# A depthwise convolution moved from 93 VectorE taps and 31 TensorE taps to 128 column-group matmuls

## What is computed

```python
def conv_module(val, gate, w_dw, b_dw, ln_g, ln_b):
    u = val * jax.nn.sigmoid(gate)                      # 512 channels
    u = lax.conv_general_dilated(u, w_dw[:, None, :], window_strides=(1,), padding=[(15, 15)],
                                 feature_group_count=512) + b_dw          # depthwise, 31 taps
    return jax.nn.silu(layernorm(u, ln_g, ln_b))        # over the 512 channels
```

## Time and profile before

| | us |
|---|---|
| median of three timed runs | 1810.6 (1808.02 to 1812.49) |
| the profiled execution, own time | 1805.73 |
| span of its trace | 1804.0 |
| PE busy in the span | 1754.0 (97%) |
| DVE busy | 1133.6 (63%) |
| ACT busy | 622.3 (34%) |
| POOL busy | 94.5 (5%) |

### The profile page before, as it was taken

One profiled execution on the slowest core, in us unless ns is written; L12 is line 12 of the kernel. 1 busy time (PEld: TensorE's weight loads), 2 busy tenths in 40 slices (PEclk: granted clock), 3 DMA queues, 4 the chain that ended last, 5 costly groups with the idle time before them and its releaser, 6 DMA issues.

```text
span 1804.0 us, 23419 instructions
## 1 busy us (share of the span) xinstructions
PE 1754.0 (97%) x9247; PEld 1469.9 (81%) x9247; DVE 1133.6 (63%) x1736; ACT 622.3 (34%) x842; POOL 94.5 (5%) x164
## 2 busy tenths in 40 slices
PE   8999999999998999999999999999999999899997
PEld 5888888888645788888888888888888989899997
DVE  5578667876885657866787577323346446665554
ACT  5322222233575432212223322122223333454343
POOL 0010000110120001000010000000000000000000
PEclk8999999999999999999999999999999999999999
DMA  9455555552101245555655353232222222245553
GB/s 392 163 196 174 188 166 198 173 181 96 45 7 42 70 140 195 176 187 166 197 173 165 119 196 128 96 114 93 73 92 94 71 71 94 94 163 170 181 170 110
DMA packets 49040, 253.36 MB, mean 140 GB/s; under 512 B 5568, under 2 KB 7104, under 8 KB 32576
## 3 DMA queue, kind: packets, MB, share of 16 engines
q1 hardware_dynamic: 30384, 184.10, 29.8%
q0 software_dynamic: 18576, 68.17, 12.1%
HBM read 251.20 MB, written 1.05 MB: 140 GB/s over the span
## 4 chain that ended last, share of the span: by engine, by line
PE 91%; DVE 4%; ACT 3%; DMA 1%; issue 1%; SPq 0%; ACTq 0%; DVEq 0%
PE ps L521 28%; PE ps L523 28%; PE ps L522 28%; PE ps L924 1%; DVE w_lo L1412 1%; PE ps L953 1%; ACT w_hi L1056 1%; PE ps L580 1%; DMA mod_raw<-in_mod_first 1%; DVE t_ring L1482 1%; PE ps L771 1%; DVE hn_lo L1489 0%; PE ps L551 0%; PE ps L785 0%; PE ps L757 0%
## 5 line engine op out<-in xcount | busy, mean ns | idle before, releaser
L521 PE MATMUL ps<-hn_hi,w_hi 128*128 128x512 f32 (+2 forms) x1784 | 643.9, 361 | 10.5 <-DVE hn_lo L1489 7.5
L523 PE MATMUL ps<-hn_hi,w_lo 128*128 128x512 f32 (+2 forms) x1784 | 637.4, 357 | 0.0
L522 PE MATMUL ps<-hn_lo,w_hi 128*128 128x512 f32 (+2 forms) x1784 | 637.3, 357 | 0.0
L1412 DVE TENSOR_TENSOR w_lo<-raw,w_hi 128x2048 fp32r<-128x2048 f32 (+2 forms) x179 | 365.6, 2042 | 334.9 <-ACT w_hi L1056 334.7
L1056 ACT ACTIVATE w_hi<-raw 128x2048 fp32r<-128x2048 f32 (+2 forms) x179 | 307.0, 1715 | 713.9 <-PE ps L523 710.6
L521 PEld LDWEIGHTS ps<-hn_hi,w_hi 128*128 128x128 f32 (+1 forms) x1784 | 337.1, 189 | 68.2 <-DVE hn_lo L1489 10.1
L523 PEld LDWEIGHTS ps<-hn_hi,w_lo 128*128 128x128 f32 (+1 forms) x1784 | 337.0, 189 | 49.7
L522 PEld LDWEIGHTS ps<-hn_lo,w_hi 128*128 128x128 f32 (+1 forms) x1784 | 337.2, 189 | 47.7 <-issue 0.5
L521 PE MATMUL ps<-a_hi,w_hi 128*128 128x512 f32 (+1 forms) x704 | 255.4, 363 | 1.7 <-DVE a_lo L1558 1.7
L522 PE MATMUL ps<-a_lo,w_hi 128*128 128x512 f32 (+1 forms) x704 | 255.2, 362 | 0.0
L523 PE MATMUL ps<-a_hi,w_lo 128*128 128x512 f32 (+1 forms) x704 | 255.2, 362 | 0.0
(11 more groups left out here) (220 smaller groups left out, 1264.5 us busy)
## 6 DMA issues: line engine op xcount, KB each, us to landing
raw<-in_w_up SPq DMA_DIRECT2D x88, 1024.0 KB, 5.0
mod_raw<-in_mod_w POOLq DMA_DIRECT2D x128, 512.0 KB, 3.9
raw<-in_w_downA SPq DMA_DIRECT2D x32, 768.0 KB, 4.2
raw<-in_w_downB SPq DMA_DIRECT2D x32, 640.0 KB, 3.9
raw<-in_w_od_in SPq DMA_DIRECT2D x16, 1024.0 KB, 5.0
mod_raw<-in_mod_first SPq DMA_DIRECT2D x8, 1024.0 KB, 11.9
raw<-in_w_ev_in SPq DMA_DIRECT2D x7, 1024.0 KB, 4.9
raw<-in_w_ev_out SPq DMA_DIRECT2D x4, 1024.0 KB, 5.0
```

What stands on the lines that cost most here:

```text
L521: pe.matmul(o, lh, rh, start=first, stop=False)
L522: pe.matmul(o, lh, rl, start=False, stop=False)
L523: return pe.matmul(o, ll, rh, start=False, stop=last)
L1412: dve.tensor_tensor(w_lo[:, u0 % 2, 0:n], raw[:, u0 % 2, 0:n], w_hi[:, u0 % 2, 0:n], ALU.subtract).then_inc(lo_made, 1)
```

## The change

All four channel tiles of the convolution go to PE, in another form, and DVE and ACT no longer compute it.

- **Form.** A tile of 128 channels is cut in four groups g of 32 channels. For group g the 128 rows of the array hold 4 taps by 32 channels, its 32 columns the 32 output channels. Group g writes PSUM partitions 32g to 32g+31, so that the four groups use the four column groups of the array. Eight steps i cover 4 x 8 = 32 taps (the 32nd is zero): step i takes tap 8q+i from row block q. So a tile is 8 x 4 = 32 matmuls of 128 rows, 32 columns and 512 moving columns; four tiles are 128 matmuls.
- **Shifted copies.** Row block q of group g needs the group's 32 channels shifted by 8q. SP makes them with DMAs inside SBUF: 16 per tile (`shift_tile`), each 32 partitions x 2 streams x 263 floats (67,328 bytes), into `mod_raw`, two tiles deep. SP issues them for tile 0 after the load of unit E+4, for tile 1 after that of E+5, and for tiles 2 and 3 after the second load of the output projection, behind waits on `conv_mm` 1 and 2 (a tile's last matmul).
- **Weights.** POOL lays each tile's taps out as [128, 32, 32] with one product of an identity and the taps (`lay_taps`, four instructions instead of 31).
- **PE.** `conv_part(n)` replaces `conv_turn(n)` at the same place: two steps (8 matmuls) in each of the 16 loop steps.
- **Copy out.** DVE copies each tile from PSUM with the bias (`conv_out`) at j = 5, 9, 13 and 17.
- **Rows of the conditioning vectors.** `mod_raw` must be free meanwhile, so POOL stops at row 54 (before: 60), and loads rows 54 to 59 after the last tile's matmuls.

```diff
-        EARLY = 30
-        TAP_ORDER = [(n % 2, n // 2) for n in range(EARLY + 12)]
-        for _n in range(10):
-            TAP_ORDER += [(2, 2 * _n), (0, 21 + _n), (2, 2 * _n + 1), (1, 21 + _n)]
-        TAP_ORDER += [(2, _n) for _n in range(20, CONV_W)]
-        TAPS = len(TAP_ORDER)
-        TAP_AT = {tap: n for n, tap in enumerate(TAP_ORDER)}
-        AHEAD_OF_LOOP = EARLY + 11
...
+        SHIFTS = TAP_ROWS * 2 * REACH
+        flat = mod_raw[:].rearrange("p a b -> p (a b)")
+
+        def shifted_place(c):
+            at = c % 2 * SHIFTS
+            return flat[:, at:at + SHIFTS].rearrange("p (g s n) -> p g s n", g=4, s=2)
+
+        def taps_place(c):
+            place = wide[:, 0:2, :].rearrange("p a b -> p (a b)") if c % 2 == 0 else flat[:, 2 * SHIFTS:2 * SHIFTS + 1024]
+            return place.rearrange("p (g i j) -> p g i j", g=4, i=TAP_STEPS)
+
+        def conv_bank(c):
+            return 1 if c % 2 == 0 else 3
+
+        def conv_parts(j):
+            return range(2 * (j - 1), 2 * j) if 1 <= j <= len(ATT) else range(0)
...
+            def shift_tile(c):
+
+                sp.wait_ge(unit_evac, U["ev_in"] + (1, 2, 6, 7)[c])
+                sp.wait_ge(pad_clear, 1)
+                if c >= 2:
+                    sp.wait_ge(conv_mm, c - 1)
+                for g in range(4):
+                    for q in range(TAP_ROWS):
+                        at = q * TAP_STEPS
+                        sp.dma_start(shifted_place(c)[32 * q:32 * q + 32, g], upad[32 * g:32 * g + 32, c, :, at:at + REACH])\
+                            .then_inc(shifted[c % 2], 16)
+
             for i in range(2, 7):
                 load(U["ev_in"] + i, 0, 0, t["w_ev_in"][i], UNIT)
+                if i == 4:
+                    sp.wait_ge(mod_made, KT + MOD_F0)
+                if i in (4, 5):
+                    shift_tile(i - 4)
             for i in range(4):
                 load(U["ev_out"] + i, 0, 0, t["w_ev_out"][i], UNIT)
+                if i == 1:
+                    shift_tile(2)
+                    shift_tile(3)
...
-            for i in range(SLOTS_MOD, MOD_F0 + SLOTS_MOD):
+            for i in range(SLOTS_MOD, MOD_F0):
...
+            def lay_taps(c):
+
+                eye = col("eye", 0, 32).unsqueeze(1).to_broadcast([P, 32, 32])
+                taps = col("conv_w", 32 * c, 32).unsqueeze(2).to_broadcast([P, 32, 32])
+                pool.tensor_tensor(taps_place(c).rearrange("p g i j -> p (g i) j"), eye, taps, ALU.mult)\
+                    .then_inc(taps_laid, 1)
+
             pool.wait_ge(rstd_mm, 2)
-            for n in range(CONV_W):
-                if n >= DIAGS:
-                    pool.wait_ge(turned_tap, n - DIAGS + 1)
-                pool.tensor_scalar(diag_place(n), ident, col("conv_w", n * CT + 3), None, ALU.mult).then_inc(diag_ready, 1)
-            for i in range(MOD_F0 + SLOTS_MOD, NMOD):
-                pool.wait_ge(mod_made, KT + i - SLOTS_MOD + 1)
+            lay_taps(0)
+            pool.wait_ge(mod_made, KT + MOD_F0)
+            lay_taps(1)
+            for c in range(2, CT):
+                pool.wait_ge(conv_mm, c - 1)
+                lay_taps(c)
+            pool.wait_ge(conv_mm, CT)
+            for i in range(MOD_F0, NMOD):
+                if i >= MOD_F0 + SLOTS_MOD:
+                    pool.wait_ge(mod_made, KT + i - SLOTS_MOD + 1)
                 vector_rows(i)
...
+            def conv_part(n):
+
+                c, i = n // TAP_STEPS, n % TAP_STEPS
+                if i == 0:
+                    if c == 0:
+                        pe.wait_ge(unit_evac, E + 7)
+                    if c >= 2:
+                        pe.wait_ge(conv_made, c - 1)
+                    pe.wait_ge(taps_laid, c + 1)
+                    pe.wait_ge(shifted[c % 2], 16 * 16 * (c // 2 + 1))
+                for g in range(4):
+                    last = pe.matmul(ps[32 * g:32 * g + 32, conv_bank(c), :], taps_place(c)[:, g, i, :],
+                                     shifted_place(c)[:, g, :, i:i + LAT], start=(i == 0), stop=(i == TAP_STEPS - 1))
+                if i == TAP_STEPS - 1:
+                    last.then_inc(conv_mm, 1)
 
             def mean_sum(c):
-                if c < 3:
-                    pe.wait_ge(tap_done, TAP_AT[c, CONV_W - 1] + 1)
-                else:
-                    pe.wait_ge(conv_made, 1)
+                pe.wait_ge(conv_made, c + 1 if c == 3 else 3)
                 return pe.matmul(ps[:, 1, :], ones, y[:, c, :], start=(c == 0), stop=(c == CT - 1))
...
-                if j == NJ + 1:
-                    act.wait_ge(turned_tap, CONV_W)
-                    act.activation(y[:, 3, :], ps[:, 3, :], ACT.Identity, bias=col("conv_b", 3)).then_inc(conv_made, 1)
...
+            def conv_out(c):
+                dve.wait_ge(conv_mm, c + 1)
+                dve.tensor_scalar(y[:, c, :], ps[:, conv_bank(c), :], col("conv_b", c), None, ALU.add).then_inc(conv_made, 1)
...
-                taps(taps_by(j - 1), taps_by(j))
+                if j >= 5 and (j - 5) % 4 == 0 and (j - 5) // 4 < CT:
+                    conv_out((j - 5) // 4)
```

More of the change, by code:

```diff
@@ L25 @@
 PAD = (CONV_W - 1) // 2
-PADDED = LAT + 2 * PAD
+TAP_ROWS = 4
+TAP_STEPS = 8
+PADDED = LAT + TAP_ROWS * TAP_STEPS
+REACH = LAT + TAP_STEPS - 1
 CT = 4
@@ L109, in build @@
         sq = sb("sq", [P, 2, TOK])
[L110 to L112 removed]
+        wide = sb("wide", [P, 3, TOK])
+        acc, sd, rstd = wide[:, 0, :], wide[:, 1, :], wide[:, 2, :]
         inv = sb("inv", [P, 2, 4])
@@ L202, in build @@
         ev_in = sem("ev_in")
-        tap_done = sem("tap_done")
-        diag_ready = sem("diag_ready")
-        turned_tap = sem("turned_tap")
+        shifted = [sem("shifted0"), sem("shifted1")]
+        taps_laid = sem("taps_laid")
+        conv_mm = sem("conv_mm")
         conv_made = sem("conv_made")
@@ L823, in _ @@
                     score(j + 1, 1)
-                for n in turned_taps(j):
-                    conv_turn(n)
+                for n in conv_parts(j):
+                    conv_part(n)
                 if 2 <= j < NJ + 1:
@@ L1624, in gated_value @@
                                   ALU.mult).then_inc(unit_evac, 1)
-            def taps(a, b):
-                for n in range(a, b):
-                    c, i = TAP_ORDER[n]
-                    if i == 0 and c in (0, 2):
-                        dve.wait_ge(unit_evac, E + 2 if c == 0 else E + 6)
-                    dst, src = two_streams(y[:, c, :]), upad[:, c, :, i:i + LAT]
-                    if i == 0:
-                        ins = dve.tensor_scalar(dst, src, col("conv_w", c), col("conv_b", c), ALU.mult, ALU.add)
-                    else:
-                        dve.wait_ge(tap_done, TAP_AT[c, i - 1] + 1)
-                        ins = dve.scalar_tensor_tensor(out=dst, in0=src, scalar=col("conv_w", i * CT + c), in1=dst,
-                                                       op0=ALU.mult, op1=ALU.add)
-                    ins.then_inc(tap_done, 1)
+            def conv_out(c):
+                dve.wait_ge(conv_mm, c + 1)
+                dve.tensor_scalar(y[:, c, :], ps[:, conv_bank(c), :], col("conv_b", c), None, ALU.add).then_inc(conv_made, 1)
             for c in range(2):
@@ L1663, in _ @@
                     rest_of(E + 4 + n)
-                taps(EARLY * n // 3, EARLY * (n + 1) // 3)
                 for i in range(2 * n, min(2 * n + 2, 5)):
@@ L1671, in _ @@
             link(dve.tensor_scalar(att_cols[:, 4, 0:NH_ATT], col("sink", 0, NH_ATT), -1.0, None, ALU.mult))
-            taps(EARLY, EARLY + 3)
             gated_value(2, t_ring[:, 0, :], bank(E + 5))
@@ L1700, in _ @@
             largest(0)
-            taps(EARLY + 3, EARLY + 5)
             largest(1)
             denominator(0)
-            taps(EARLY + 5, AHEAD_OF_LOOP)
             gated_value(3, t_ring[:, 1, :], bank(E + 6))
@@ L2016, in layout @@
     put["c_in"] = cond.reshape(P, KT * 32)
+    taps = np.zeros((TAP_ROWS * TAP_STEPS, CT * P), np.float32)
+    taps[:CONV_W] = np.asarray(ev_conv_w).reshape(CONV_W, CT * P)
+    taps = taps.reshape(TAP_ROWS, TAP_STEPS, CT, 4, 32).transpose(0, 4, 2, 3, 1).reshape(P, CT * 32)
     put["cols"] = np.concatenate(
         [columns(ffn1_norm), columns(mix_norm), columns(ffn2_norm), columns(final_norm), columns(ev_conv_b),
-         columns(ev_conv_ln_g), columns(ev_conv_ln_b), columns(od_norm_g), columns(ev_conv_w), columns(mod_b),
-         np.broadcast_to(ev_sink.reshape(1, -1), (P, NH_ATT)), np.broadcast_to(od_b_gate.reshape(1, -1), (P, 4 * HM))],
+         columns(ev_conv_ln_g), columns(ev_conv_ln_b), columns(od_norm_g), taps, columns(mod_b),
+         np.broadcast_to(ev_sink.reshape(1, -1), (P, NH_ATT)), np.broadcast_to(od_b_gate.reshape(1, -1), (P, 4 * HM)),
+         np.tile(np.eye(32, dtype=np.float32), (4, 1)), np.zeros((P, 12), np.float32)],
         axis=1)
```

18 lines of the change are left out of this document (2 added, 16 removed).

## The result

The changed kernel takes 1821.4 us (median of 5, 1819.52 to 1824.98) where the kernel before takes 1810.1 (1808.02 to 1812.49) on the same chip. The measured ratio is 1.0073, 95% interval 1.0063 to 1.0084; the two medians by themselves give the lower end of it. They are 11.4 us apart, against a forecast of 0.5 us less, and outside the range. The profiled execution of the changed kernel took 1821.42 us, span 1819.6, 15.6 over that of before.

The account below looks back on a forecast made before the run. It took PE as holding 91% of the chain, with PE or ACT's ring pacing the loop except one DVE-late step. -1.0 + 0.5 = -0.5 us gave 1810.1 us from a median of 1810.6; range 1803.5 to 1815.

Parts of the forecast that it names:

- DVE's late step: Attention loop, step 14: without taps on DVE its late largest score falls back from 7.09 to 6.08 us, gaining 1.0 us.
- 64 rounds against 62, side by side: PE's convolution: four column groups overlap, so 64 rounds replace 62 passes; the added two are hidden in step 16.
- the price of the form: PE entering and leaving the column-group form: 0.1 us in each of five loop steps without idle time, 0.5 us in all.
- SP and the shifted copies: SP's queue: 64 DMAs and the loads behind them stay hidden, cost 0.
- The 0.94: Input projection: the us per SP issue up to which the load of unit E+6 is still in time.
- the sharing rival: PE's convolution: groups share something at 512 columns, a round takes 0.58 us, total 1813.0; chance 0.05.
- stopped-up SP: SP's queue: small DMAs cost over 0.94 us each, the load of E+6 is late, 1828 at 1.5 us per issue; chance 0.07.
- groups one behind the other: PE's convolution: groups don't overlap, 256 passes against 62, 89 us more, 1899; chance 0.02.
- POOL, 0: POOL's four tap products: those of tiles 2 and 3 have 21.7 us in the loop, so cost 0.
- 4.9 I allowed: POOL: the us estimated for one tap product, in proportion to the old 612 ns diagonals.
- I count no change of clock: Input projection and attention loop: granted clock 1.00 in both and PE gets no less work, so no clock term.
- a wait that my list lacks: Anywhere, such as a tile's copy landing after its step: over 5.4 us slower, 1818; chance 0.03.

Follow-up runs that it names:

- a1: The changed kernel with 16 more unused columns behind `cols`, so `a_hi`, `a_lo` and `mod_raw` begin at a multiple of 128 bytes again; 1812.92 us, ratio 1.0026 to before.
- a2: The kernel before with 48 unused columns in `cols`, so its buffers stand at the changed kernel's addresses; 1817.32 us, ratio 1.0050 to before.
- b2: The kernel before with 32 unused columns (128 bytes) in `cols`, moving everything behind it; executed once, span 1816.7 us.
- c3: The kernel before with only `w_hi` and `w_lo` moved by 64 bytes, the other buffers keeping their place modulo 256; executed once, span 1830.0 us.
- c1: The changed kernel with `a_hi` back in place, plus four half-size products on POOL behind its first two at the second norm; executed once, span 1808.4 us.
- e1: The changed kernel with `a_hi` back in place and 18 instead of 4 filling matmuls on PE at the second norm; executed once, second norm to first score 77.23 us.
- a3: The changed kernel with POOL's first two tap products moved behind the evacuation of unit E+1 of the input projection; 1816.70 us, ratio 1.0048 to before.

## Why the prediction was wrong

- **DVE's late step, -1.0 us: right.** 6.10 us from turn to turn against 6.08 forecast, and ACT's wait for DVE is gone. Of the loop's idle time otherwise nothing went: the waits for ACT are 0.42 and 0.60 us, where they were 0.36 and 0.55.
- **64 rounds against 62, side by side: right, and so is the price of the form.** Sixteen passes take 1.85 us for 1.83, and the turn behind them 0.66 for 0.60, so up to 0.08 us a step for the 0.1 that I took. A period of four steps takes 553.47 - 533.95 = 19.52 us for 543.23 - 523.89 = 19.34; two periods make 0.4 us of the 0.5 in the sum. With the 1.0 of the late step that is the 0.6 that the loop gained.
- **SP and the shifted copies, 0: right.** 0.74 and 0.64 us an issue, landing in 2.1 us; PE waited for no copy. The 0.94 at which they would have come late was not reached. A round takes 0.46 us, where the sharing rival had 0.58. The rivals of a stopped-up SP, of sharing groups and of groups one behind the other didn't occur.
- **POOL, 0: the step that failed.** I asked of tiles 2 and 3 whether their products are ready in time, and a product takes 1.9 us, well under the 4.9 I allowed. What I did not ask is who stands beside the products of tiles 0 and 1: they begin at the second norm, where DVE's `hn_lo` is the next thing that PE needs. In the trace of before the only sign of it is small: the pair takes 0.99 us beside the old diagonals of 0.6 us, where later pairs take 0.87 to 0.96. It cost 5.6 us in the trace, half of it through the clock. "I count no change of clock" was wrong with it: PE got no less work, but a gap of 3.5 us.
- **The address of the moving columns: a term that isn't in the sum at all.** The diff makes the parameter table `cols` 48 columns longer, and my list of the parts of the change has no entry for it, so it went in at nothing without a reason. It moves every buffer allocated behind it, and that is 10.6 us in the down projections by the traces, 8.5 to 9.0 by the timed executions of a1 and a2. No row of the kernel before shows such a cost, since all its operands stand alike; the rival "a wait that my list lacks" (0.03, 1818) is the only place where it could have been, with a time near the measured one (1818 for 1821) and another mechanism; it got too little.

## What to carry to other kernels

A diff that changes the size of a buffer changes the address of every buffer behind it. Where PE is full, keep moving columns and weights alike modulo 256 bytes, and check the interval from matmul to matmul in stages that the diff does not touch. And when work moves to POOL, ask first not whether it is done in time, but which DVE instructions with two SBUF operands run beside it, and whether PE waits for them: in these traces two long products there cost 2.7 us of waiting, and many short diagonals 0.1.

## What the runs showed of the hardware

- 512-column matmuls follow each other in 226.7 ns with moving columns and weights at the same place modulo 256 bytes, and in 233.3 ns with the moving columns 32 or 128 bytes ahead of the weights or 64 behind (eight kernels with buffers moved). In b2 the intervals alternate between 229 and 238 ns, in c3 between 231 and 236.
- Column groups of 32 with 128 rows and 512 columns run four abreast: sixteen passes in 1.85 us, where four one by one take 1.83, and the full matmuls behind them start 0.06 us later.
- A gap of 3.5 us on PE was followed by half clock (1.2 GHz) for 3.4 us in c1 and 6.8 us in a1 and the changed kernel; filled with 18 matmuls (e1) it was followed by none. Gaps of 0.75 to 0.81 us at the same place (before, a3) were followed by none.
